# Moving page loads between the queues of a decoder-step kernel, and a threshold chain inside a projection

## The chip, the cores and the metric

The kernel is one program on one core of a Trainium2 chip. The metric is the device time of one execution in microseconds (us), lower is better. TensorE (PE) multiplies, VectorE (DVE) and ScalarE (ACT) do elementwise work, GpSimd (POOL) does elementwise work too, and SyncE (SP) computes nothing: it issues transfers. Here SP, ScalarE and GpSimd all issue transfers from their own instruction streams, and an engine that issues a transfer does nothing else during that time.

## The reference, cut to what matters

The program is one inference step of a two-layer decoder for a prompt (1024 tokens) and for 8 sample sequences of 8 new tokens each. Only the sample part of the sparse attention (DSA) in layer 0 is touched:

```python
def dsa_sample(layer, q, k_new, v_new, iq, ik_new, iw, cache_k, cache_v, cache_idx, page_table):
    ik_past = cache_idx[layer, page_table].reshape(Bd, PAST_LEN, IDX_DIM)   # 8 x 16 pages of 128 keys
    ik_all = jnp.concatenate([ik_past, ik_new], axis=1)
    sc = indexer_scores(iq, iw, ik_all)            # sum over 8 heads of weight * relu(iq . ik)
    _, idx = lax.top_k(sc, 256)                    # the 256 best of 2056 keys for each query
    ...
    return dsa_attend(q, ks, vs, idx <= t)         # softmax attention over the chosen keys
```

The pages of keys, values and index keys lie in a pool in HBM, and `page_table` says which page belongs where. The kernel doesn't gather the 256 keys: it finds the threshold (with ties counted), makes a bias of 0 or -1e30 for each of the 2056 keys, and attends to all of them under this bias.

## The kernel before, in words

Each stage of the program is a block: every engine runs its own instruction list, and all five meet at a barrier at the block's end. Three blocks matter.

**First block of `even_in` (line 266).** The input projection x @ w_in is cut into 12 chunks of weight columns, `PROJ`; this block multiplies the first `CW` = 9 of them. Each chunk has `KD` = 8 blocks of 128 input rows, and each block is 5 units on TensorE (two token tiles to a unit, the last unit has one): 360 units in all. For every block ScalarE makes the high part of the weights (`split_hi`, L207) and VectorE the low part (`split_lo`, L212) into a ring of `RING` = 4 slots. The helper `projection(n)` on VectorE or ScalarE emits the splits and evictions that are due when TensorE is at unit n: a split for block g once block g - 3 is reached. So the order in which VectorE's work stands between the splits is written out by hand. Between the units TensorE also computes the sample's index scores: for 16 steps m it transposes pages of index keys (L404), two sequences to four steps (`ix_in[b]` says that the 16 pages of sequence b have landed), multiplies them with the queries (L413) and adds the heads (L420). Then VectorE searches the 256 largest scores of each half row in 32 rounds (L513, L514), with `projection` calls between the rounds; it ends at unit `SEARCH` + 128 = 321. GpSimd then exchanges the two halves' lists (L360, semaphore `oth_in`), and VectorE makes the bias in a chain of 17 operations (L523 to L541), each waiting for the one before. GpSimd stores the bias to DRAM (L362) and waits for it (`b_out`). In this block the SP queue loads the weights of the chunks (`load_w`, L182), stores chunks 0 and 1 from a buffer of four slots (`store_stage`, L187), and loads the index pages of sequences 3 and 5; GpSimd loads those of 0, 1, 2, 4, 6 and 7.

**Second block of `even_in` (line 581)** multiplies the last three chunks beside the prompt's linear attention (GLA).

**`dsa_sample` (block at line 1592)** attends for the sample. Sequences go in four pairs p. For each pair TensorE transposes the key pages (`keys_T`, L1645) into two banks that ScalarE and VectorE empty (`copy_keys`, L1587), computes the scores with the bias (L1664, L1667), then already transposes the keys of the next pair, then transposes the probabilities (L1681) and multiplies the values (L1696, L1697). For each sequence there are 16 key pages and 16 value pages of 64 KB. `load_pages` (L54) loads them: in a loop over groups of four it reads four page numbers out of the page table into registers (`value_load`, L57) and issues four transfers (L61). The key pages of sequences 0, 2, 4, 6 and 7 and the value pages of 6 and 7 are on SP; those keys of 1, 3 and 5 are on ScalarE (`load_odd`), between its copies; the values of 0 to 5 are on GpSimd. Key and value buffers have four slots, so from sequence 4 on a load waits until the slot's old pages were transposed (`kt_done`) or multiplied (`y_done`). SP also loads the spread matrix, the bias and the new values between its keys.

Of the kernel before, what the change touches and what calls it, by code (L numbers as in the profile page):

```python
# [17 lines left out]
KD = D // P  # L18
# [18 lines left out]
TOPK = 256  # L37
# [4 lines left out]
PAGES = 16  # L42
# [10 lines left out]

def load_pages(eng, pages, n_pool, b, j0, j1, cache, dst_of, landed):  # L54
    group = 4
    with eng.Fori(j0 // group, j1 // group) as g:
        at = [eng.value_load(pages[0:1, bass.ds(g * group + (b * PAGES + r), 1)], min_val=0, max_val=n_pool - 1) for r in range(group)]  # L57
        for r in range(group):
            src = cache[bass.ds(at[r], 1)]
            src = src.rearrange("o p k d -> (o p) (k d)") if len(src.shape) == 4 else src.rearrange("o p d -> (o p) d")  # L60
            eng.dma_start(dst_of(bass.ds(g * group + r, 1)), src).then_inc(landed, 16)  # L61
# [40 lines left out]
def even_in(nc, st, A, C, O, x_tile, H, Hs):  # L102
# [35 lines left out]
    with ExitStack() as ctx:  # L138
# [127 lines left out]
        with ExitStack() as early, nc.Block() as block:  # L266
# [27 lines left out]
            def index_slot(p):  # L294
                return (idxb[:, 0], idxb[:, 1], staged_keys, idxb[:, 0])[p]

            def load_index(eng, b, j0, j1):
                load_pages(eng, pages, n_pool, b, j0, j1, A["cache_idx"][0],
                           lambda j: index_slot(b // 2)[:, j, b % 2, :].rearrange("p o d -> p (o d)"), ix_in[b])

# [5 lines left out]
            def _(sp):  # L306
# [15 lines left out]
                for c in range(1, CW + 1):  # L322
                    load_w(sp, c)
                    if c == 1:
                        sp.wait_ge(t_done, 2 * TILES)
                        load_index(sp, 3, 0, PAGES)
# [4 lines left out]
                    if c == 3:  # L331
                        sp.wait_ge(evac, NB * 3)
                        sp.dma_start(scr_w, Hs[0:NS, C_IW:C_IW + 8]).then_inc(w_out, 16)
                        sp.wait_ge(w_out, 16)
                        for f in range(2):
                            for h in range(8):
                                sp.dma_start(iwd[NS * f + 8 * h:NS * f + 8 * h + 8, :],
                                             bass.AP(scr_w.tensor, NS * f + h, [[8, 8], [2 * NS, NB2]]),
                                             allow_slow_non_contiguous=True).then_inc(iw_in, 16)
                        wait_staged(sp)  # L340
                        load_index(sp, 5, 0, PAGES // 2)
                    elif c == 4:
                        load_index(sp, 5, PAGES // 2, PAGES)
                sp.wait_ge(cin, 96)

            @block.gpsimd
            def _(pool):
                pool.wait_ge(pin, 16)
                load_index(pool, 0, 0, PAGES)
                load_index(pool, 1, 0, PAGES)  # L350
                pool.wait_ge(t_done, 2 * TILES)
                load_index(pool, 2, 0, PAGES)
                wait_staged(pool)
                load_index(pool, 4, 0, PAGES)
                pool.wait_ge(it_done, NQ)
                load_index(pool, 6, 0, PAGES)
                load_index(pool, 7, 0, PAGES)
                pool.wait_ge(lst_done, 1)
                for f in range(2):
                    pool.dma_start(oth[NS * f:NS * f + NS, :], lst[NS * (1 - f):NS * (1 - f) + NS, :]).then_inc(oth_in, 16)  # L360
                pool.wait_ge(b_done, 1)
                pool.dma_start(st.bias_dram, bias[:, :]).then_inc(b_out, 16)  # L362
                pool.wait_ge(b_out, 16)

# [112 lines left out]
            def _(dve):  # L477
# [38 lines left out]
                dve.sem_inc(lst_done, 1)  # L516
                projection(NB * KD * CW)
                for k in range(RING):
                    split_lo(dve, nc.vector.tensor_tensor, CW, k)
                dve.wait_ge(oth_in, 32)  # L520
# [13 lines left out]
                link(nc.vector.reduce_sum(more[:, :], hit[:, :], AX_X))  # L534
                link(nc.vector.tensor_tensor(num[:, :], num[:, :], more[:, :], ALU.subtract))
                equal, count = wk[:, :], relb[:, :, :].rearrange("p a n -> p (a n)")
                link(nc.vector.tensor_scalar(equal, sc[:, :], thr[:, 0:1], None, ALU.is_equal))
                link(nc.vector.tensor_tensor_scan(count, ones[:, 0:1].to_broadcast([P, LH]), equal, 0.0, ALU.mult, ALU.add))
                link(nc.vector.scalar_tensor_tensor(out=equal, in0=count, scalar=num[:, 0:1], in1=equal, op0=ALU.is_le, op1=ALU.mult))
                link(nc.vector.scalar_tensor_tensor(out=equal, in0=sc[:, :], scalar=thr[:, 0:1], in1=equal, op0=ALU.is_gt, op1=ALU.add))  # L540
                nc.vector.tensor_scalar(bias[:, :], equal, -1.0, -NEG, ALU.add, ALU.mult).then_inc(b_done, 1)  # L541

        gsb = lambda n, s, d=F32: ctx.enter_context(nc.sbuf_tensor(f"gla_{n}", s, d))
# [996 lines left out]
def dsa_sample(nc, st, A, C, O, Hs, XT):  # L1540
# [7 lines left out]
    with ExitStack() as ctx:  # L1548
# [39 lines left out]

        def load(eng, b, j0, j1, cache, dst, slot, landed):
            load_pages(eng, pages, n_pool, b, j0, j1, cache, lambda j: dst[:, slot, j, :].rearrange("p o c -> p (o c)"), landed)  # L1590

        with nc.Block() as block:
            @block.sync
            def _(sp):
                sp.dma_start(pages[:, :], A["page_table"].rearrange("(o a) b -> o (a b)", o=1)).then_inc(pin, 16)
                sp.wait_ge(pin, 16)
                load(sp, 0, 0, PAGES, A["cache_k"][0], Kp, 0, k_in[0])
                for f in range(2):
                    sp.dma_start(spf[NS * f:NS * f + NS, :, :], C["spread"]).then_inc(cin, 16)
                sp.dma_start(bias[:, :], st.bias_dram).then_inc(bias_in, 16)  # L1600
                for b in range(NB):
                    sp.dma_start(Vn[:, b, :], Hs[8 * b:8 * b + 8, C_DV:C_DV + P]).then_inc(vn_in, 16)
                for b in (2, 4, 6, 7):
                    if b >= 4:
                        sp.wait_ge(kt_done, 4 * (b - 3))
                    load(sp, b, 0, PAGES, A["cache_k"][0], Kp, b % 4, k_in[b % 4])
                sp.wait_ge(y_done, NP_ - 2)
                for b in range(NB - 2, NB):
                    load(sp, b, 0, PAGES, A["cache_v"][0], Vp, b % 4, v_last_in[b % 2])

            @block.gpsimd
            def _(pool):
                pool.wait_ge(pin, 16)
                for b in range(4):
                    load(pool, b, 0, PAGES, A["cache_v"][0], Vp, b % 4, v_in[b % 4])
                for p in range(NP_):
                    pool.wait_ge(y_done, p + 1)
                    for b2 in range(2):
                        pool.dma_start(bass.AP(scr_y.tensor, (2 * p + b2) * DEC_SEQ * 512, [[HD, 8], [512, DEC_SEQ], [1, HD]]),
                                       yq[64 * b2:64 * b2 + 64, p, :]).then_inc(y_out, 16)  # L1620
                        if p + 3 < NP_:
                            load(pool, 2 * p + 4 + b2, 0, PAGES, A["cache_v"][0], Vp, (2 * p + b2) % 4, v_in[(2 * p + b2) % 4])
                pool.wait_ge(y_out, 32 * NP_)
# [82 lines left out]
            def _(act):  # L1706
# [7 lines left out]
                act.wait_ge(h_c, 3)  # L1714
                act.wait_ge(pin, 16)

                def load_odd(b, j0, j1):
                    if b >= 4 and j0 == 0:
                        act.wait_ge(kt_done, 4 * (b - 3))
                    load(act, b, j0, j1, A["cache_k"][0], Kp, b % 4, k_in[b % 4])  # L1720

                load_odd(1, 0, PAGES)

# [5 lines left out]
                new_keys(0)  # L1729
                load_odd(3, 0, PAGES)  # L1730
                for g in range(8):
                    copy_keys(act, nc.scalar.copy, g)
                for p in range(NP_):
# [5 lines left out]
                    if p + 1 < NP_:  # L1739
                        act.wait_ge(s_done, p + 1)  # L1740
                        new_keys(p + 1)
                        for g in range(8 * p + 8, 8 * p + 16, 2):
                            copy_keys(act, nc.scalar.copy, g)
                        if p == 0:
                            load_odd(5, 0, PAGES)
                act.wait_ge(yt_done, 1)
# [1361 lines left out]
```

## Time and profile before

| | us |
|---|---|
| median of 3 runs | 3800.31 (3798.08 to 3800.9) |
| the profiled execution | 3798.53, span 3796.9 |
| first block of `even_in`, from its first projection product | 34.7 to 340.7 of the span |
| second block of `even_in` | 340.7 to 627.7 |
| `dsa_sample` | 627.7 to 814.6 |
| prompt attention, `dsa_out` | 814.6 to 1513 |
| the rest: feed-forward twice, odd layer | 1513 to 3796.9 |
| TensorE busy over the span | 3327.2 (88%) |
| VectorE, ScalarE, GpSimd busy | 42%, 29%, 10% |

In the timeline a row gives the start, the length, the engine, the line and the operation, with `out<-in` in the program's names; what stands in brackets is the time that the engine sat idle before it and who ended that. A row with x16 merges 16 instructions, and its length runs from the first one's start to the last one's end. SPq, ACTq and POOLq are the engines' instruction queues.

### The profile page before, as it was taken

The page shows a single profiled execution, that of the slowest core. Times are in us where ns is not written, and L with a number is a line of the kernel's source. Part 1 is how long each engine was busy: PE and PEld are TensorE (multiplying, and loading weights), DVE is VectorE, ACT ScalarE, POOL GpSimd, SP SyncE. Part 2 cuts the span into 40 slices and gives each one's busy share as a digit, 9 for nine tenths or more (in the row PEclk, how much of TensorE's full clock was granted, in tenths as well). Part 3 has the DMA queues.
Part 4 walks back from the last instruction along what each step waited for, and adds up shares of the span by engine and source line. Part 5 has one row for each costly group of instructions (what it writes and reads, how often), then busy time and mean ns, then how long its engine had stood idle before and what let it go on. Part 6 is the DMA issues. An engine that isn't in the chain of part 4 may idle for free. (4 is left out here: it accounts for less than half of the span.)

```text
span 3796.9 us, 53619 instructions
## 1 busy us (share of the span) xinstructions
PE 3327.2 (88%) x20601; PEld 2834.1 (75%) x20627; DVE 1601.5 (42%) x2851; ACT 1095.4 (29%) x2144; POOL 394.2 (10%) x507
## 2 busy tenths in 40 slices
PE   8996884668878887999999998896997999999997
PEld 7796674434444443999999998893665999999997
DVE  2184762216777782211112565331554211112566
ACT  2223442122333332211112443212443211112443
POOL 2200112321111100000000001350000000000002
PEclk9998885867788887999999999896999999999999
DMA  4111004440000000111112110213001111112111
GB/s 139 45 34 30 23 12 129 113 146 12 20 20 20 12 12 28 50 44 44 44 44 93 40 56 34 52 54 111 20 34 39 45 44 44 44 44 91 40 58 48
DMA packets 232358, 190.76 MB, mean 50 GB/s; under 512 B 49538, under 2 KB 210580, under 8 KB 232148
## 3 DMA queue, kind: packets, MB, share of 16 engines
q1 hardware_dynamic: 216436, 166.17, 14.5%
q0 software_dynamic: 8832, 19.02, 1.6%
q10 hardware_dynamic: 6912, 3.15, 0.3%
q8 instruction: 118, 1.93, 0.2%
q14 instruction: 60, 0.49, 0.0%
HBM read 158.64 MB, written 31.38 MB: 50 GB/s over the span
## 5 line engine op out<-in xcount | busy, mean ns | idle before, releaser
L1885 PE MATMUL ffn1u_ps<-h_hi,ffn1u_whi 128*128 128x384 f32 (+1 forms) x1056 | 348.5, 330 | 8.7 <-DVE h_lo L1947 8.7
L1885 PE MATMUL ffn0u_ps<-h_hi,ffn0u_whi 128*128 128x384 f32 (+1 forms) x1056 | 344.9, 327 | 8.6 <-DVE h_lo L1947 8.6
L1885 PE MATMUL ffn1u_ps<-h_lo,ffn1u_whi 128*128 128x384 f32 (+1 forms) x1056 | 348.3, 330 | 0.0
L1885 PE MATMUL ffn1u_ps<-h_hi,ffn1u_wlo 128*128 128x384 f32 (+1 forms) x1056 | 348.3, 330 | 0.0
L1885 PE MATMUL ffn0u_ps<-h_hi,ffn0u_wlo 128*128 128x384 f32 (+1 forms) x1056 | 345.1, 327 | 0.0
L1885 PE MATMUL ffn0u_ps<-h_lo,ffn0u_whi 128*128 128x384 f32 (+1 forms) x1056 | 344.9, 327 | 0.0
L196 PE MATMUL ine_ps<-ine_w_hi,ine_x_hi 128*128 128x256 f32 (+2 forms) x864 | 264.9, 307 | 4.6 <-DVE ine_w_lo L212 4.6
L196 PE MATMUL ine_ps<-ine_w_hi,ine_x_lo 128*128 128x256 f32 (+2 forms) x864 | 250.3, 290 | 0.0
L196 PE MATMUL ine_ps<-ine_w_lo,ine_x_hi 128*128 128x256 f32 (+2 forms) x864 | 249.6, 289 | 0.0
L1885 PEld LDWEIGHTS ffn1u_ps<-h_hi,ffn1u_whi 128*128 128x128 f32 x1056 | 199.2, 189 | 9.1 <-DVE ffn1u_wlo L1929 9.1
L1885 PEld LDWEIGHTS ffn0u_ps<-h_hi,ffn0u_whi 128*128 128x128 f32 x1056 | 198.7, 188 | 8.9 <-DVE ffn0u_wlo L1929 8.9
L1885 PEld LDWEIGHTS ffn1u_ps<-h_lo,ffn1u_whi 128*128 128x128 f32 x1056 | 199.1, 189 | 0.0
L1885 PEld LDWEIGHTS ffn1u_ps<-h_hi,ffn1u_wlo 128*128 128x128 f32 x1056 | 199.1, 189 | 0.0
L1885 PEld LDWEIGHTS ffn0u_ps<-h_hi,ffn0u_wlo 128*128 128x128 f32 x1056 | 198.6, 188 | 0.0
L1885 PEld LDWEIGHTS ffn0u_ps<-h_lo,ffn0u_whi 128*128 128x128 f32 x1056 | 198.6, 188 | 0.0
L2033 PE MATMUL ffn0d_ps<-ffn0d_w_hi,ffn0d_a_hi 128*128 128x256 f32 (+1 forms) x594 | 171.6, 289 | 12.9 <-DVE ffn0d_X L2135 6.5
L2033 PE MATMUL ffn1d_ps<-ffn1d_w_hi,ffn1d_a_hi 128*128 128x256 f32 (+1 forms) x594 | 171.2, 288 | 12.9 <-DVE ffn1d_X L2135 6.5
L196 PEld LDWEIGHTS ine_ps<-ine_w_hi,ine_x_hi 128*128 128x128 f32 (+1 forms) x864 | 167.2, 194 | 17.3 <-issue 8.6
L196 PEld LDWEIGHTS ine_ps<-ine_w_hi,ine_x_lo 128*128 128x128 f32 (+1 forms) x864 | 167.4, 194 | 4.1 <-issue 4.1
L2033 PE MATMUL ffn0d_ps<-ffn0d_w_hi,ffn0d_a_lo 128*128 128x256 f32 (+1 forms) x594 | 170.1, 286 | 0.0
L2033 PE MATMUL ffn0d_ps<-ffn0d_w_lo,ffn0d_a_hi 128*128 128x256 f32 (+1 forms) x594 | 170.0, 286 | 0.0
L2033 PE MATMUL ffn1d_ps<-ffn1d_w_hi,ffn1d_a_lo 128*128 128x256 f32 (+1 forms) x594 | 169.7, 286 | 0.0
(441 smaller groups left out, 7418.2 us busy)
## 6 DMA issues: line engine op xcount, KB each, us to landing
ffn0u_raw<-in_ffn_w_gu_dram SPq DMA_DIRECT2D x44, 512.0 KB, 3.8
ffn1u_raw<-in_ffn_w_gu_dram SPq DMA_DIRECT2D x44, 512.0 KB, 3.8
ffn0d_w<-in_ffn_w_down_dram SPq DMA_DIRECT2D x88, 128.0 KB, 2.1
ffn1d_w<-in_ffn_w_down_dram SPq DMA_DIRECT2D x88, 128.0 KB, 2.2
smp_Vp<-in_cache_v_dram POOLq DMA_DIRECT2D x96, 64.0 KB, 2.2
ine_w<-in_w_in_even_dram SPq DMA_DIRECT2D x5, 1024.0 KB
scratch_h<-ine_stage SPq DMA_DIRECT2D x20, 256.0 KB, 2.5
smp_Kp<-in_cache_k_dram SPq DMA_DIRECT2D x80, 64.0 KB, 2.0
```

The source lines that it names most:

```text
L196: last = nc.tensor.matmul(o, xp[:, k, i * P:i * P + r], wp[:, g % RING, 0:n], start=(k == 0 and j == 0 and i % 2 == 0), stop=(k == KD - 1 ...
L1885: last = nc.tensor.matmul(ps[:, t, k2, 0:n], wp[:, k2, k, :], hp[:, k, t0:t0 + n], start=(k == 0 and j == 0), stop=(k == KD - 1 and j == 2))
L2033: last = nc.tensor.matmul(acc(i), ap[:, n % 2, i * P:i * P + rows(i)], wp[:, k, :], start=(k == 0 and j == 0 and i % 2 == 0), stop=(k == K ...
```

## The change

The threshold chain of 17 VectorE operations is cut in two and put among the splits of the ninth chunk (`CW` - 1), instead of after all of them. The bias is stored to DRAM by SP, not by GpSimd. The index pages of sequences 1 and 7 move from GpSimd to SP, and GpSimd loads its own in groups of one page. In `dsa_sample` SP issues all key pages; ScalarE issues none.

```diff
-def load_pages(eng, pages, n_pool, b, j0, j1, cache, dst_of, landed):
-    group = 4
+def load_pages(eng, pages, n_pool, b, j0, j1, cache, dst_of, landed, group=4):
...
             def _(sp):
...
                     if c == 1:
+                        load_index(sp, 1, 0, PAGES)
                         sp.wait_ge(t_done, 2 * TILES)
                         load_index(sp, 3, 0, PAGES)
...
                     elif c == 4:
                         load_index(sp, 5, PAGES // 2, PAGES)
+                        sp.wait_ge(it_done, NQ)
+                        load_index(sp, 7, 0, PAGES)
+                sp.wait_ge(b_done, 1)
+                sp.dma_start(st.bias_dram, bias).then_inc(b_out, 16)
+                sp.wait_ge(b_out, 16)
                 sp.wait_ge(cin, 96)
             def _(pool):
                 pool.wait_ge(pin, 16)
-                load_index(pool, 0, 0, PAGES)
-                load_index(pool, 1, 0, PAGES)
+                load_index(pool, 0, 0, PAGES, 1)
                 pool.wait_ge(t_done, 2 * TILES)
-                load_index(pool, 2, 0, PAGES)
+                load_index(pool, 2, 0, PAGES, 1)
                 wait_staged(pool)
-                load_index(pool, 4, 0, PAGES)
+                load_index(pool, 4, 0, PAGES, 1)
                 pool.wait_ge(it_done, NQ)
-                load_index(pool, 6, 0, PAGES)
-                load_index(pool, 7, 0, PAGES)
+                load_index(pool, 6, 0, PAGES, 1)
...
-                pool.wait_ge(b_done, 1)
-                pool.dma_start(st.bias_dram, bias[:, :]).then_inc(b_out, 16)
-                pool.wait_ge(b_out, 16)
...
                 dve.sem_inc(lst_done, 1)
-                projection(NB * KD * CW)
-                for k in range(RING):
-                    split_lo(dve, nc.vector.tensor_tensor, CW, k)
+                projection(SEARCH + 4 * (TOPK // 8) + NB)
                 dve.wait_ge(oth_in, 32)
...
                 link(nc.vector.tensor_tensor(num[:, :], num[:, :], more[:, :], ALU.subtract))
+                projection(SEARCH + 4 * (TOPK // 8) + 3 * NB)
...
                 nc.vector.tensor_scalar(bias[:, :], equal, -1.0, -NEG, ALU.add, ALU.mult).then_inc(b_done, 1)
+                projection(NB * KD * CW)
+                for k in range(RING):
+                    split_lo(dve, nc.vector.tensor_tensor, CW, k)
...
                 load(sp, 0, A["cache_k"][0], Kp, 0, k_in[0])
+                load(sp, 1, A["cache_k"][0], Kp, 1, k_in[1])
...
-                for b in (2, 4, 6, 7):
+                for b in range(2, NB):
...
-                act.wait_ge(pin, 16)
-                def load_odd(b, j0, j1):
-                    if b >= 4 and j0 == 0:
-                        act.wait_ge(kt_done, 4 * (b - 3))
-                    load(act, b, j0, j1, A["cache_k"][0], Kp, b % 4, k_in[b % 4])
-                load_odd(1, 0, PAGES)
                 new_keys(0)
-                load_odd(3, 0, PAGES)
...
-                        if p == 0:
-                            load_odd(5, 0, PAGES)
```

## Rows read from the trace of the kernel before

**Rows 1.** Stage table: length, busy time (x instructions) by engine, granted clock, DMA share, GB/s.
```profile
34.70:340.70 306.00, 274.35 (x2097) 249.51 (x2097) 132.76 (x213) 61.98 (x165) 42.38 (x79) 0.96 0.19 50
627.70:814.60 186.90, 98.56 (x581) 69.39 (x581) 34.75 (x62) 21.79 (x40) 56.65 (x105) 0.76 0.34 95
```
**Rows 2.** Timeline of TensorE where the first block ends.
```profile
340.78 0.37 PE L632 MATMUL ine_ps<-ident,H 128*16 128x128 f32 x1 [24.75 <-PEq L266]
```
**Rows 3.** Timeline of VectorE there: last splits, and three of the chain's 17 operations.
```profile
316.95 1.43 DVE L212 TENSOR_TENSOR ine_w_lo<-ine_w,ine_w_hi 128x256 fp32r<-128x256 f32 x4 [12.87 <-ACT ine_w_hi L207]
318.30 0.28 DVE L523 COPY idx_rel<-idx_rel 128x256 f32<-128x256 f32 x1
...
322.56 0.76 DVE L537 TENSOR_SCALAR idx_wk<-idx_sc,idx_thr 128x1032 f32<-128x1032 f32 x1
...
328.35 0.70 DVE L541 TENSOR_SCALAR idx_rel<-idx_wk 128x1032 bf16<-128x1032 f32 x1
```
**Rows 4.** Timeline of GpSimd: the lists' exchange and the bias's store.
```profile
298.98 1.07 POOL L360 DMA_DIRECT2D idx_rel<-idx_lst  x2 [118.20 <-DVEq L516]
329.35 0.59 POOL L362 DMA_DIRECT2D scratch_bias<-idx_rel  x1 [29.30 <-DVE idx_rel L541]
```
**Rows 5.** Line 266, the block's end (duration ns min/median/max, first and last start us).
```profile
L266 POOLq DRAIN  x1: 8149/8149/8149, 332.3 to 332.3; - x1
```
**Rows 6.** Timeline of TensorE: first products of blocks 69 and 71.
```profile
306.23 0.28 PE L196 MATMUL ine_ps<-ine_w_hi,ine_x_hi 128*128 128x256 f32 x1
...
312.66 0.28 PE L196 MATMUL ine_ps<-ine_w_hi,ine_x_hi 128*128 128x256 f32 x1
```
**Rows 7.** Timeline of TensorE: the thirteenth transpose of index pages.
```profile
182.31 0.63 PE L404 MATMUL ine_ps<-ident,idx_keys 128*128 128x128 f32 x4 [2.32 <-DMA idx_keys<-in_cache_idx_dram]
```
**Rows 8.** Timeline of GpSimd: four pages of index keys of sequence 6.
```profile
144.43 2.47 POOL L61 DMA_DIRECT2D idx_keys<-in_cache_idx_dram  x4 [2.90 <-issue]
```
**Rows 9.** Timeline of SP's queue in the first block.
```profile
37.05 19.39 SPq L61 DMA_DIRECT2D idx_keys<-in_cache_idx_dram  x16
60.15 2.52 SPq L187 DMA_DIRECT2D scratch_h<-ine_stage  x4
62.71 2.76 SPq L182 DMA_DIRECT2D idx_w<-in_w_in_even_dram  x3
```
**Rows 10.** Tile idx_w, loads from 62 to 66 us.
```profile
DMA to landing us min/median/max: 3.5/4.6/4.9
```
**Rows 11.** Timeline of ScalarE: it evicts the second chunk.
```profile
85.24 2.74 ACT L233 COPY ine_stage<-ine_ps 128x512 f32<-128x512 f32 x4 [0.39 <-PE ine_ps L196]
```
**Rows 12.** Timeline of SP's queue in `dsa_sample`.
```profile
632.07 17.37 SPq L61 DMA_DIRECT2D smp_Kp<-in_cache_k_dram  x16
...
651.49 5.54 SPq L1602 DMA_DIRECT2D smp_Vn<-Hs  x8
660.30 18.35 SPq L61 DMA_DIRECT2D smp_Kp<-in_cache_k_dram  x16
...
746.23 18.37 SPq L61 DMA_DIRECT2D smp_Vp<-in_cache_v_dram  x16
...
767.66 19.59 SPq L61 DMA_DIRECT2D smp_Vp<-in_cache_v_dram  x16
```
**Rows 13.** Line 57 in `dsa_sample`: a page number is read.
```profile
L57 SPq TENSOR_LOAD <-smp_pages x112: 262/264/598, 629.2 to 784.1; - x112
```
**Rows 14.** DMA issues in `dsa_sample`: line, count, KB each, median us to landing.
```profile
smp_Vp<-in_cache_v_dram SPq DMA_DIRECT2D x32, 64.0 KB, 1.9
```
**Rows 15.** Timeline of TensorE in `dsa_sample`.
```profile
672.88 0.48 PE L1645 MATMUL smp_ps<-ident,smp_Kp 128*128 128x128 f32 x1 [19.58 <-ACT smp_KT L1587]
...
766.23 6.28 PE L1696 MATMUL smp_ps<-smp_Vp,smp_PT 128*64 128x128 f32 x32 [4.94 <-DMA smp_Vp<-in_cache_v_dram]
...
793.99 3.71 PE L1696 MATMUL smp_ps<-smp_Vp,smp_PT 128*64 128x128 f32 x32
797.63 0.43 PE L1697 MATMUL smp_ps<-smp_Vn,smp_PT 8*64 8x128 f32 x2
```

More of the change, by code:

```diff
@@ L295, in index_slot, with load_index @@
                 return (idxb[:, 0], idxb[:, 1], staged_keys, idxb[:, 0])[p]
-            def load_index(eng, b, j0, j1):
+            def load_index(eng, b, j0, j1, group=4):
                 load_pages(eng, pages, n_pool, b, j0, j1, A["cache_idx"][0],
-                           lambda j: index_slot(b // 2)[:, j, b % 2, :].rearrange("p o d -> p (o d)"), ix_in[b])
+                           lambda j: index_slot(b // 2)[:, j, b % 2, :].rearrange("p o d -> p (o d)"), ix_in[b], group)
             def wait_staged(eng):
@@ L1587, in copy_keys, with load @@
             op(KT[:, g // 4 % 2, 512 * (g % 4):512 * (g % 4 + 1)], ps[:, 5 + g % 2, :]).then_inc(key_copy(g)[0], 1)
-        def load(eng, b, j0, j1, cache, dst, slot, landed):
-            load_pages(eng, pages, n_pool, b, j0, j1, cache, lambda j: dst[:, slot, j, :].rearrange("p o c -> p (o c)"), landed)
+        def load(eng, b, cache, dst, slot, landed):
+            load_pages(eng, pages, n_pool, b, 0, PAGES, cache, lambda j: dst[:, slot, j, :].rearrange("p o c -> p (o c)"), landed)
         with nc.Block() as block:
@@ L1596, in _ @@
                 sp.wait_ge(pin, 16)
-                load(sp, 0, 0, PAGES, A["cache_k"][0], Kp, 0, k_in[0])
+                load(sp, 0, A["cache_k"][0], Kp, 0, k_in[0])
+                load(sp, 1, A["cache_k"][0], Kp, 1, k_in[1])
                 for f in range(2):
@@ L1602, in _ @@
                     sp.dma_start(Vn[:, b, :], Hs[8 * b:8 * b + 8, C_DV:C_DV + P]).then_inc(vn_in, 16)
-                for b in (2, 4, 6, 7):
+                for b in range(2, NB):
                     if b >= 4:
                         sp.wait_ge(kt_done, 4 * (b - 3))
-                    load(sp, b, 0, PAGES, A["cache_k"][0], Kp, b % 4, k_in[b % 4])
+                    load(sp, b, A["cache_k"][0], Kp, b % 4, k_in[b % 4])
                 sp.wait_ge(y_done, NP_ - 2)
                 for b in range(NB - 2, NB):
-                    load(sp, b, 0, PAGES, A["cache_v"][0], Vp, b % 4, v_last_in[b % 2])
+                    load(sp, b, A["cache_v"][0], Vp, b % 4, v_last_in[b % 2])
             @block.gpsimd
@@ L1614, in _ @@
                 for b in range(4):
-                    load(pool, b, 0, PAGES, A["cache_v"][0], Vp, b % 4, v_in[b % 4])
+                    load(pool, b, A["cache_v"][0], Vp, b % 4, v_in[b % 4])
                 for p in range(NP_):
@@ L1621, in _ @@
                         if p + 3 < NP_:
-                            load(pool, 2 * p + 4 + b2, 0, PAGES, A["cache_v"][0], Vp, (2 * p + b2) % 4, v_in[(2 * p + b2) % 4])
+                            load(pool, 2 * p + 4 + b2, A["cache_v"][0], Vp, (2 * p + b2) % 4, v_in[(2 * p + b2) % 4])
                 pool.wait_ge(y_out, 32 * NP_)
```

## The prediction

> **What bounds the kernel now.** I read the stage table first, to see where TensorE isn't the limit. The line to notice is `dsa_sample`: 186.9 us with TensorE busy for 98.6, while VectorE, ScalarE and GpSimd are each busy for 57 us or less, and the transfers' share is 0.34 [rows 1]. No engine's work and no bandwidth fills this stage, so something that the busy columns don't count does. In the first block TensorE is busy 274 of 306 us [rows 1]; there only holes are to be won. Then I read the timeline at the first block's end: TensorE sat idle for 24.75 us until the second block began at 340.78 [rows 2]. Walk back from there. GpSimd's instruction queue shows a DRAIN of 8.15 us from 332.3 to 340.45 [rows 5]. Before that it stored the bias, issued at 329.35 and waited for until 332.3 [rows 4, 5]. The bias came from VectorE's chain, 318.30 to 329.05, and this stood behind the last weight splits, which ended at 318.38 [rows 3]. So the hole is a chain of splits, threshold chain, store, and drain. Last, I read SP's queue in `dsa_sample`: it goes from one batch of 16 pages to the next without a pause [rows 12].
>
> **The threshold chain.** It moves into the ninth chunk. It needs the exchanged lists, issued by 300.05 [rows 4]; with the 1.9 us that a 64 KB transfer takes to land [rows 14], about 302, and the rest of the window up to 316 has VectorE nearly empty. Its first part (12 operations) takes 318.30 to 322.56 = 4.3 us, its second 322.56 to 329.05 = 6.5 us [rows 3]. Started at 301.5 to 302, the first part ends at 306. Now the splits: with `projection(326)` block 68 is split ahead of it, 69 and 70 follow it, 71 follows the second part. TensorE reaches block 69 at 306.23 and block 71 at 312.66 [rows 6]. 69 is just in time, or late by 0.2. The second part runs from 306.5 to 313.0, and block 71's split (four took 1.43 [rows 3]) comes at 313.4: TensorE waits 0.8 us. All later work of the block moves by 0.8, so the last split ends at 319.2. SP has nothing else to do by then; its store of the bias begins at 313.1 and is confirmed by 316.1, taking the 3 us of GpSimd's [rows 4, 5]. GpSimd's last transfer is now the exchange at 300.05, and its drain of 8.15 us, if it is as long there, ends near 309, under the products. The barrier took 0.33 from the drain's end to TensorE's start [rows 2, 5]. TensorE starts at 319.5 and not at 340.8: **-21.3 us**. The idle time shrinks from 24.75 to some 3. Value products after 4.94 us of idle took 6.28, those without 3.71 [rows 15], so the first products of the second block may win 0 to 2.6; I take -1.0, since a short idle time shows it too.
>
> **Index pages.** TensorE waited 2.32 us at its thirteenth step for the pages of sequence 7, which GpSimd loaded last [rows 7]. Now SP issues them behind sequence 5's, some 20 us before they are needed, and GpSimd ends with sequence 6. It pays for a group of one: four pages took 5.37 us (2.47 + 2.90) [rows 8], and has 12 more loop turns for 16 pages. In the 2.90 us four page numbers are read, at no less than SP's 0.264 each [rows 13], and one turn is made, so a turn costs between 0 and 1.8; I take an estimate of 0.5, since the reads need register operations too, and a batch is 6 us longer. Sequence 6, begun at 136.2 and 21.5 long, would end by 164, 16 us before step 13; at 1.8 a turn it would end at 179 and the gain would be gone. I take **-2.3 us**. But SP is moved past its own stores and weights. After sequence 1's pages (in the place of 3's, to 56.44) it issues those of 3, 21.7 us more (below): to 78.2. Only then come the stores of chunk 0, before at 60.15, and the weights of chunk 2, before at 62.71 [rows 9]. Four stores whose data is ready take 2, the three weight issues 2.76: to 82.9, landed at 86.4 to 87.8 by 3.5 to 4.9 us each [rows 10]. ScalarE's program has the first splits of chunk 2 ahead of its evictions of chunk 1, which began at 85.24 [rows 11]. It would begin them three splits (0.3 each) after landing, at 87.5. TensorE needs the first bank when it is through chunk 1, at about 87.7, with the copy of 0.6 to 0.7 done: a wait of 0.4 in the middle, 0 to 3.5 at the bounds. I take **+0.5**. The stores of chunk 0 land by 84, ahead of those evictions, which need their slots.
>
> **Key pages.** ScalarE issued 48 pages in three batches and held up its copies; the row to see is TensorE's wait of 19.58 us for a copy, until 672.88 [rows 15]. That stall goes. What is late next is the same moment: sequence 1's keys now come second on SP, ending at 649.44 + 21.7 = 671.2 and landing at 673. So nothing is won for the first pair, and three batches are added to SP. What does a batch cost on this queue? From the last issue of sequence 2 (678.65) to the last of value sequence 7 (787.25) SP issued 5 batches without a wait: 108.6 / 5 = 21.72 us, 1.36 a page [rows 12]. This is instruction time: reading one page number takes 0.264 us for the load alone [rows 13], and register operations and the issue come on top. SP's list is then: sequence 0 to 649.44 as before, sequence 1 to 671.2, spread, bias and new values 7.6 (649.44 to 657.03) to 678.8, and 8 batches more (keys 2 to 7, values 6 and 7), 173.8, to 852.5. Before it was 787.25, so +65.2. Its waits (`kt_done`, `y_done` at 2) are long met then: keys of 6 would be issued from 765, when those of sequence 2, landed at 702, are transposed. Sequence 7's keys land at 811; transposes, the third pair's probabilities and values, the fourth's scores and softmax are some 37 us more as in the timeline of before, to 848 or so, and the last value pages land at 852.5 + 1.9 = 854.4 [rows 14]. So these are last. In the trace of before they weren't: landed at 789.2, and their product began at 793.99 [rows 12, 15]. After the wait that product takes 6.3 + 0.3 [rows 15] and ends at 861.0 instead of 798.06: **+62.9 us**. GpSimd's value pages, waiting on pair 0's and 1's products, fall back too but land 25 us before their use. The tail of the stage is unchanged.
>
> **A rule weighed.** The row shows 21.7 us for 16 pages of 64 KB [rows 12], each landing in 1.9 [rows 14]: issue, not movement. The Trainium skill, page "DMA: Bandwidth & Descriptors", section "Issuing engines are not separate DMA queues", says that issuing on several engines at once saves only the sequencer's time, "usually small relative to the DMA itself". By that rule the batches moved would cost nothing, which is the second rival below. The trace speaks against it in this case.
>
> **The sum.** On the profiled execution: 3798.5 - 21.3 - 1.0 - 2.3 + 0.5 + 62.9 = 3837.3. The median of the runs is 1.8 above that execution, so 3839.
>
> **The rivals.**
> 1. *The queue runs faster alone.* If ScalarE's issues slowed SP's, ten batches would take 17.37 + 3.27 = 20.6 each (the shortest length, and 657.03 to 660.30 before it [rows 12]); SP ends at 843: 3829. Against it: from 746.23 to 767.66 ScalarE issued nothing, and the pitch was 21.4 [rows 12].
> 2. *Not slower: the key pages are hidden.* The place is the last value pages on SP. If SP had slack of over 63 us there, or the copies freed on ScalarE gave it back, the stage would keep its length: 3839 - 62.9 = 3776. It decides once a batch costs under about 8 us (the gain of 24 over three). For it speaks only the stall of 19.58 [rows 15]; against it the unbroken queue.
> 3. *Weights of chunk 2 late.* Landing 4 us later adds 4 and some products at the lower clock, up to +7: 3846.
> 4. *The drain or the store ends the block after all.* If GpSimd's drain begins only when the others are done, 8 of the 21.3 come back: 3847; if none of the hole goes, 3860.
>
> **Chances.** My forecast 0.71 (3832 to 3846), rival 1 0.10, rival 3 0.07, rival 4 0.07, rival 2 0.05. The range: below, rival 1 with a margin for the clock, 3826; above, rivals 3 and most of 4, 3851. A difference under about 0.2% (8 us) can't be told from none here. Slower than that 0.94, within it 0.02, faster 0.04.
>
> **What would show it.** TensorE's idle time before L632 of 3 us; a wait of some 0.8 before the last block's products; no wait at the thirteenth L404; SP's page transfers in `dsa_sample` as ten batches at a pitch of 21.7 without pauses; TensorE waiting on `smp_Vp` from SP at the end, and on `smp_Kp` before each pair from the second on. I am wrong if SP shows pauses there, if a batch takes well under 20 us, or if the stage ends by anything else.

## The result, and the profile after

The changed kernel takes **3838.97 us** (median; 3836.47 to 3862.03), against 3799.19 of the kernel before (3790.54 to 3800.9, measured beside it): a ratio of 1.0122 with a 95% interval of 1.0086 to 1.0157: slower, by 1.2%. A second comparison gave 3837.37 against 3798.3, 1.0107 (1.0093 to 1.0122). The prediction was 3839. The profiled execution took 3838.52, with a span of 3836.9 against 3796.9, so 40.0 us are to be found.

The stage table of after, for the same two stages as [rows 1] (start and end, length, busy time by engine, granted clock, DMA share, GB/s):

```profile
34.70:316.00 281.30, 274.04 (x2097) 249.14 (x2097) 132.79 (x214) 61.41 (x165) 26.45 (x50) 0.99 0.21 55
602.90:852.90 250.00, 108.69 (x581) 76.69 (x581) 35.23 (x62) 22.07 (x40) 56.68 (x105) 0.66 0.25 71
```

TensorE did the same work in the first block (274 us), in 281 us instead of 306. In `dsa_sample` it did the same instructions in 250 us instead of 187; its busy time grew by 10, with a mean granted clock of 0.66 instead of 0.76 of full speed. The engine waits more, and works slower after waits (the same 32 products took 6.58 us behind a wait, below, and 3.71 elsewhere).

**The first block's end.** Timelines of VectorE, TensorE, SP's queue and GpSimd, and the line of GpSimd's DRAIN, the last instruction of its list in a block (duration ns, then first and last start):

```profile
298.06 0.29 DVE L521 COPY idx_rel<-idx_rel 128x256 f32<-128x256 f32 x1 [2.02 <-DMA idx_rel<-idx_lst]
...
302.34 0.76 DVE L211 TENSOR_TENSOR ine_w_lo<-idx_w,ine_w_hi 128x256 fp32r<-128x256 f32 x2
303.02 0.75 DVE L536 TENSOR_SCALAR idx_wk<-idx_sc,idx_thr 128x1032 f32<-128x1032 f32 x1
...
308.80 0.70 DVE L540 TENSOR_SCALAR idx_rel<-idx_wk 128x1032 bf16<-128x1032 f32 x1
309.42 0.42 DVE L211 TENSOR_TENSOR ine_w_lo<-idx_w,ine_w_hi 128x256 fp32r<-128x256 f32 x1
...
314.28 1.43 DVE L211 TENSOR_TENSOR ine_w_lo<-ine_w,ine_w_hi 128x256 fp32r<-128x256 f32 x4 [4.45 <-ACT ine_w_hi L206]
```
```profile
309.89 0.39 PE L195 MATMUL ine_ps<-ine_w_hi,ine_x_hi 128*128 128x256 f32 x1 [0.37 <-DVE ine_w_lo L211]
316.05 0.27 PE L634 MATMUL ine_ps<-ident,H 128*16 128x128 f32 x1 [2.69 <-PEq L265]
```
```profile
309.52 0.34 SPq L347 DMA_DIRECT2D scratch_bias<-idx_rel  x1
```
```profile
295.61 1.06 POOL L363 DMA_DIRECT2D idx_rel<-idx_lst  x2 [136.11 <-DVEq L516]
```
```profile
L265 POOLq DRAIN  x1: 6080/6080/6080, 296.1 to 296.1; - x1
```

The chain now stands among the splits and is over at 309.5, while TensorE still multiplies. TensorE's idle time before the second block is 2.69 us where [rows 2] had 24.75. The DRAIN still takes 6.08 us, but from 296.1 on, beside the products. The second block begins at 316.05 and not at 340.78: 24.7 us won.

**`dsa_sample`.** SP's queue, then the waits of TensorE (us in total, times, longest), then its last rows:

```profile
607.27 40.13 SPq L60 DMA_DIRECT2D smp_Kp<-in_cache_k_dram  x32
...
658.25 125.77 SPq L60 DMA_DIRECT2D smp_Kp<-in_cache_k_dram  x96
787.48 40.55 SPq L60 DMA_DIRECT2D smp_Vp<-in_cache_v_dram  x32
```
```profile
PE smp_ps L1648 <- DMA smp_Kp<-in_cache_k_dram: 101.7, 7, 22.7
...
PE smp_ps L1699 <- DMA smp_Vp<-in_cache_v_dram: 5.3, 1, 5.3
```
```profile
829.51 6.58 PE L1699 MATMUL smp_ps<-smp_Vp,smp_PT 128*64 128x128 f32 x32 [5.32 <-DMA smp_Vp<-in_cache_v_dram]
836.02 0.43 PE L1700 MATMUL smp_ps<-smp_Vn,smp_PT 8*64 8x128 f32 x2
```

SP goes through ten batches without a pause (in the gaps of some 3 us it reads the first page numbers of the next group); from the end of the new values (654.99) to its last issue (828.03) the last eight took 173.0 us, 21.6 a batch. TensorE waited seven times for key pages, 101.7 us in all, and at the end for the last value pages, as forecast. From the block's first transpose to its last product it was 233.05 us (602.97 to 836.02) against 169.85 (627.78 to 797.63, [rows 15]): 63.2 lost. -24.7 + 63.2 is 38.5 of the 40.0. The other 1.5 lie behind these stages, where it can't be placed: from the first transposes of the prompt's attention to the span's end it was 2974.9 us before and 2976.6 after, and between 2972.3 and 2979.7 in the experiments, which change nothing there.

### The profile page after: what moved, and what is told of

Read it like the earlier page. It is cut to its first block and busy times, and to the rows that moved or that the text cites. A ratio compares the mean times of both kernels' runs of the same rounds, so it can differ in the third digit from the quotient of the medians.

```text
span 3836.9 us, 53726 instructions
## 1 busy us (share of the span) xinstructions
PE 3341.4 (87%) x20627; PEld 2841.1 (74%) x20627; DVE 1602.3 (42%) x2851; ACT 1095.6 (29%) x2143; POOL 376.5 (10%) x474
```

## The experiments

Each is compared with the kernel before, run beside it on the same chip.

**The two halves apart.** First the changed kernel with `dsa_sample` as before:

```diff
-                load(sp, 1, A["cache_k"][0], Kp, 1, k_in[1])
...
-                for b in range(2, NB):
+                for b in (2, 4, 6, 7):
...
+                load_odd(1, 0, PAGES)
...
+                load_odd(3, 0, PAGES)
...
+                            load_odd(5, 0, PAGES)
```


> The changed kernel with dsa_sample as it was before (key pages of sequences 1, 3 and 5 on ScalarE): the part of the change in the first block alone. My theory (two independent parts, first block -24.7 us as the trace of after shows, dsa_sample +63.2): TensorE begins the second block at 316, dsa_sample is again 170.3 us long, and the time is 3799.2 - 24.7 = 3774.5, up to 1.7 more if the small rise in the later stages comes from the first part too. Rival (the gain of the first block is given back later, because the later stages start their transfers earlier and meet other traffic or a lower clock): above 3785.

Measured: **3770.98 us** (3770.08 to 3774.68) against 3797.2, ratio 0.9932 (0.9915 to 0.9948): -26.2, 3.5 under the expected 3774.5. Then the kernel before with `dsa_sample` of after, the same edit the other way round:

> The kernel before with only dsa_sample changed: all key pages on SP. My theory: ten batches in a row on SP, +63.2 us, 3862.4. Rival (key pages are hidden, and the loss came from something else, for instance the bias or the barrier arriving at another moment): near 3799. Where the two parts add, this difference and that of the run with the first part alone sum to +39.8, the change's own.

Measured: **3857.96 us** (3856.95 to 3861.63) against 3797.2, ratio 1.0165 (1.0148 to 1.0182): +60.8 (expected: +63.2). So the change holds a gain and a loss, each in its place, and neither is given back elsewhere. The two sum to +34.6, 4.5 less than the change's own +39.1 (second comparison; 39.8 in the first). The traces show where such an amount lies: the unchanged code of `dsa_sample` took 169.85 us in the profiled execution of before, but 165.63 in the run with the first part alone, and 165.47 and 165.72 in two runs further down. In the trace of before, TensorE's wait for sequence 5's values was 4.94 us and the products behind it took 6.28 ([rows 15]), against 3.69 and 5.33 with the first part alone; the value products from 788.10 on took 5.61 against 3.71, with a granted clock of 0.70 there and 1.00 in the other. That makes 4.1 of the 4.2 us. Why the clock was lower there isn't settled; the same code took 167.17 us in the run with the bias stored by GpSimd. So against the first part alone the key pages cost 67.4 us (233.05 - 165.63), and against before 61.2 (keys-only run, 231.05) to 63.2.

**How far SP's list decides.** The last two batches of SP's list to GpSimd:

```diff
-                sp.wait_ge(y_done, NP_ - 2)
-                for b in range(NB - 2, NB):
-                    load(sp, b, A["cache_v"][0], Vp, b % 4, v_last_in[b % 2])
...
+                    if p == 1:
+                        for b in range(NB - 2, NB):
+                            load(pool, b, A["cache_v"][0], Vp, b % 4, v_last_in[b % 2])
```


> The changed kernel with the last two batches of SP's list in dsa_sample (value pages of sequences 6 and 7) issued by GpSimd after pair 1's values. SP then issues 8 batches and ends with the keys of sequence 7, at 784 as before. My theory: SP's queue sets the time twice, at each pair's keys and at the last values; with the values gone only the last wait (5.32 us) and the slower products behind it (6.58 for 3.71) are won, and the stage ends 8.2 us earlier: 3831. GpSimd's two batches end near 800 and land ahead of their use at 818. Rival A (only the length of SP's list counts, 21.7 us a batch): -43, 3796. Rival B (GpSimd's batches are later than SP's were): at or above 3839.

Measured: **3826.8 us** (3822.61 to 3845.08), ratio 1.0078 (1.0061 to 1.0095); about 11 less than the changed kernel. The stage was 223.60 us long in the trace, 9.45 less than after (expected: 8.2). Two batches of 21.6 us off the queue gave 9, because the keys of sequence 7, from the same queue, were next by 5 us. The value pages were last, but only just; what costs the 63 us is the whole row of key pages.

**Issue or transfer.** The same number of transfers of the same size, but from fixed places, so that SP reads no page number (this leaves the page table out for all key pages and the last value pages):

```diff
+            if eng is nc.sync:
+                for j in range(PAGES):
+                    src = cache[b * PAGES + j:b * PAGES + j + 1]
+                    src = src.rearrange("o p k d -> (o p) (k d)")
+                    eng.dma_start(dst[:, slot, j, :], src).then_inc(landed, 16)
+                return
```


> The changed kernel with SP's pages in dsa_sample fetched from fixed places in the caches, in the same number and size, so that no page number is read, no register is worked on and there is no loop: it leaves the page table out for the key pages and the last value pages. My theory (SP's instructions set the 1.36 us of a page): a batch of 16 takes about 8 us (0.5 each, as fixed transfers on SP elsewhere), keys are there early, and GpSimd's value pages at 23 us a batch are next: the stage ends 60 to 92 us earlier, 3747 to 3779. Rival (the transfers or their rings set the pace, not the instructions): batches of over 17 us, and 3839 or little under it.

Measured: **3769.38 us** (3768.38 to 3771.5), ratio 0.9929 (0.9912 to 0.9945). SP's queue in this run, and one of TensorE's waits:

```profile
603.78 15.52 SPq L1596 DMA_DIRECT2D smp_Kp<-in_cache_k_dram  x32
...
627.10 46.68 SPq L1596 DMA_DIRECT2D smp_Kp<-in_cache_k_dram  x96
702.07 16.09 SPq L1596 DMA_DIRECT2D smp_Vp<-in_cache_v_dram  x32
```
```profile
739.65 5.24 PE L1705 MATMUL smp_ps<-smp_Vp,smp_PT 128*64 128x128 f32 x32 [14.28 <-DMA smp_Vp<-in_cache_v_dram]
```

96 pages are issued in 46.68 us, 0.49 each instead of 1.35, and SP's ten batches now cost less than before's seven. Both the stage (165.54 us) and the time are some 68 us shorter than the changed kernel's. So neither bandwidth nor the transfers' own queues set the pace, but the 0.86 us that reading the page number, its register work and the loop add to each issue. What is left waits on GpSimd, which still reads page numbers (14.28 us before its value pages), as the expectation has it.

**The DRAIN's price.** The first part alone, with the bias stored by GpSimd again:

```diff
-                sp.wait_ge(b_done, 1)
-                sp.dma_start(st.bias_dram, bias).then_inc(b_out, 16)
-                sp.wait_ge(b_out, 16)
...
+                pool.wait_ge(b_done, 1)
+                pool.dma_start(st.bias_dram, bias[:, :]).then_inc(b_out, 16)
+                pool.wait_ge(b_out, 16)
```


> The first-block part alone (3770.98), with one piece of it undone: the bias is stored by GpSimd again, which waits for it, and not by SP. The threshold chain stays in the ninth chunk. My theory: GpSimd's DRAIN starts when its last transfer is confirmed and has a length of its own of 6 to 8.6 us. The bias is ready at 309.5, the store is confirmed at 312.5, the DRAIN ends at 318.6 to 320.7, and the second block starts there and not at 316: +2.9 to +5.0, 3774 to 3776. Rival (the DRAIN only waits for transfers that are open, so it is short once they are confirmed): no difference, 3771.

Measured: **3772.69 us** (3771.0 to 3775.8), 1.7 over the first part alone, at equal ratios (0.9932; 0.9916 to 0.9949), so the time alone doesn't decide it. The trace does:

```profile
L265 POOLq DRAIN  x1: 5536/5536/5536, 313.4 to 313.4; - x1
```
```profile
319.24 0.27 PE L634 MATMUL ine_ps<-ident,H 128*16 128x128 f32 x1 [4.93 <-PEq L265]
```

The DRAIN begins once the store is confirmed, takes 5.54 us, and the second block begins right at its end, 2.6 us later than with SP's store (316.65; expected: 2.9 to 5.0). So it has a length of its own, and with the chain already moved, the store's move is worth 2 to 3 us, not 8.

**The late weights.** The profiled execution of the run with value pages on GpSimd took 3845.08, 18 us over that kernel's median. TensorE's row where chunk 2 begins, and windows of this trace (start and end, length, busy times by engine, granted clock, DMA share, GB/s):

```profile
90.43 0.31 PE L195 MATMUL ine_ps<-ine_w_hi,ine_x_hi 128*128 128x152 f32 x1 [2.51 <-ACT ine_stage L232]
```
```profile
80.00:91.00 11.00, 8.49 (x72) 8.26 (x71) 0.77 (x3) 1.95 (x6) 0.00 (x0) 1.00 0.63 160
91.00:102.00 11.00, 11.00 (x63) 11.00 (x63) 0.95 (x3) 1.85 (x6) 2.14 (x4) 0.57 0.62 200
102.00:135.00 33.00, 33.00 (x164) 33.00 (x164) 3.00 (x8) 4.24 (x15) 6.42 (x12) 0.50 0.05 14
```

The weights of chunk 2, which SP issues behind sequence 3's pages, were late; TensorE waited 2.51 us and then worked at the lower of its two clock levels (0.50 of full speed, 1.2 GHz), from about 92.5 to 137 us. In the same 33 us the run with the first part alone, at full clock, issued 242 matmuls and not 164. To force it, sequence 3's pages in groups of one on SP (`load_index(sp, 3, 0, PAGES, 1)`), on the first part alone:

> The first-block part alone (3770.98), with sequence 3's index pages on SP read one by one (12 more loop turns of 0.43 us), so that the weights of chunk 2 behind them land 5 us later, at some 93 where they landed at 88.02. It tests what the 2.04 us wait at chunk 2 turns into. My theory, from the profiled execution of the run with value pages on GpSimd (a wait of 2.51 us there, then the granted clock at 0.50 from 91 to 136 us): every execution waits 7 us and then multiplies at the lower clock for some 45 us, +5 and +20: 3796. Rival (the clock had another cause and only the wait counts): +5, 3776.

Measured: **3769.7 us** (3768.7 to 3792.09), ratio 0.9922 (0.9906 to 0.9939): as a forced delay it failed. A loop turn cost less than I had put (the batch took 3.0 us more, not 5.2) and it began 1.8 earlier, so the weights landed at 89.52, only 1.5 later. But one of five executions, the profiled one, took 3792.09, and its trace has a wait and the same windows:

```profile
90.88 0.31 PE L195 MATMUL ine_ps<-ine_w_hi,ine_x_hi 128*128 128x152 f32 x1 [1.33 <-ACT ine_stage L232]
```
```profile
102.00:135.00 33.00, 33.00 (x164) 33.00 (x164) 2.47 (x7) 4.23 (x15) 6.75 (x13) 0.50 0.05 14
```

My "every execution" is wrong: a wait of 1.33 us was followed by the lower clock, waits of 2.04, 2.01 and 1.02 us at the same place (first part alone, index pages alone, bias on GpSimd) weren't. One thing sets the two apart in these traces: TensorE went on later, at 90.43 and 90.88 against 89.37, 90.14 and 89.74; five cases are too few to call that the reason. The cure to try is to issue the weights first:

```diff
                         load_index(sp, 1, 0, PAGES)
+                    if c == 2:
                         sp.wait_ge(t_done, 2 * TILES)
                         load_index(sp, 3, 0, PAGES)
```


> The first-block part alone (3770.98), with SP issuing the stores of chunk 0 and the weights of chunk 2 ahead of sequence 3's index pages, not behind them. The weights land near 65. My theory: the wait of 2.04 us before chunk 2's first bank goes, nothing else is late (sequence 3's pages land near 86, and TensorE needs them after 140): 3769, and no execution 20 us over the others. Rival (the pages or chunk 1's stores behind them become late): 3771 or more.

Measured: **3771.16 us** (3770.76 to 3773.86), ratio 0.9929 (0.9913 to 0.9946). SP's queue has the weights at 64.38, 16 us ahead of after's 80.80, and the wait is gone, but the 2 us of it don't show in the median: the expected 3769 missed, and the number is the rival's (3771 or more), though TensorE waits for nothing new in this block's trace. The same edit on the changed kernel, with the changed kernel beside it:

> The changed kernel itself again, as the mate of the next run. My theory: most executions within 4 us of 3838, and some (one of four so far) 20 to 24 us longer with a mean granted clock lower by 0.006, those in which the late weights of chunk 2 end in 44 us at the lower clock. Rival (the long execution of before was a chance event that has nothing to do with the weights): none here, or as many in the next run.

> The changed kernel with SP issuing the stores of chunk 0 and the weights of chunk 2 ahead of sequence 3's index pages. My theory: no wait at chunk 2, so no execution with the 44 us at the lower clock there; median 0 to 2 us under the changed kernel's. Rival (see the run of the changed kernel): long executions here too.

Measured: **3837.37 us** (3834.78 to 3838.54; ratio 1.0107, 1.0093 to 1.0122) and **3836.45 us** (3835.97 to 3838.29; 1.0105, 1.009 to 1.0119). No long execution in either, so this pair decided nothing. Counted over all runs of this study, the seven kernels with the weights behind the pages had 5 long executions of 42 (18 to 24 us over their kernel's median; 3862.03 of the changed kernel is one), the four with the weights first none of 16. Two of the five have a trace, and both show the lower clock behind that wait. With before's first block, in which the weights land in time, none of 39 was long. Five long ones among 97 would all fall among those 42 by chance in about one case of 75. But the 42 differ from the 39 in all that moving the index pages did; the fair contrast for the weights is with the 16, and five long ones among these 58 would all miss the 16 in about one case of 5. So the count doesn't settle it: that the late weights make the long executions is what the two traces point to, and it isn't shown.

**Index pages alone**, on the kernel before:

```diff
                     if c == 1:
+                        load_index(sp, 1, 0, PAGES)
...
+                        sp.wait_ge(it_done, NQ)
+                        load_index(sp, 7, 0, PAGES)
...
-                load_index(pool, 1, 0, PAGES)
...
-                load_index(pool, 7, 0, PAGES)
```


> The kernel before with the index pages alone moved (sequences 1 and 7 to SP, groups of one on GpSimd). My theory: the wait of 2.32 us at the thirteenth step goes, and the wait at chunk 2 (0 to 2 us) comes: 1.8 to 3.3 us faster than before, a ratio of 0.9991 to 0.9995, and most of the 26 us of the first-block part belongs to the threshold chain. Rival (the two edits need each other, since the bias and the lists share GpSimd's queue): over 5 us faster, or slower than before.

Measured: **3788.85 us** (3784.6 to 3813.16) against 3798.3, ratio 0.9987 (0.9974 to 1.0001): 9 us by the medians, with an interval that takes in none at all. The expectation (1.8 to 3.3) missed, and the medians lie where the rival had them (over 5 us), though the trace shows other reasons for it. The trace places 4.87 us in the first block: its VectorE chain begins 2.05 earlier, as expected, and GpSimd's DRAIN took 5.54 us where [rows 5] had 8.15, which I hadn't expected. Another 4.4 are the shorter `dsa_sample` (165.47), whose code is that of before; with 12 and 17 executions behind the two medians this is more than one trace's chance, but what would tie it to the edit isn't shown. The second block begins thus:

```profile
335.91 0.37 PE L632 MATMUL ine_ps<-ident,H 128*16 128x128 f32 x1 [21.93 <-PEq L265]
```

Of the 24.7 us of the first block, then, some 4.9 are the index pages' and some 20 the chain's and the store's.

**Another DRAIN, and the queues dealt out anew.** On the run with the weights first, the last pair's y goes by SP, which also reads all of y back at the end:

```diff
-                for p in range(NP_):
+                for p in range(NP_ - 1):
                     pool.wait_ge(y_done, p + 1)
...
+                sp.wait_ge(y_done, NP_)
+                for b2 in range(2):
+                    sp.dma_start(bass.AP(scr_y.tensor, (2 * NP_ - 2 + b2) * DEC_SEQ * 512, [[HD, 8], [512, DEC_SEQ], [1, HD]]),
+                                 yq[64 * b2:64 * b2 + 64, NP_ - 1, :]).then_inc(y_last_out, 16)
```


> As the run with the weights first, and in dsa_sample the last pair's two stores of y and the load that reads them back go to SP, so that GpSimd's last transfer is pair 2's store. My theory: GpSimd's DRAIN of 8.6 us, which ends the block of dsa_sample in the trace of before and of after, begins some 35 us earlier and is hidden; the next block starts 7 to 8.6 us sooner: 3760.5 to 3762 (against 3769). Rival (other engines' ends, or the transfers that the next block starts with, are as late): 3767 to 3769.

Measured: **3763.3 us** (3761.71 to 3764.26), ratio 0.9906 (0.989 to 0.9923), 7.9 less than without the edit. GpSimd's DRAIN at this block's end was 9.12 us long and began at 747.8, ahead of the last products; SP's, at 775.6, took 7 ns. TensorE's wait before the next block's first transposes, without the edit and with it:

```profile
794.01 1.97 PE L1207 MATMUL dsa_ps<-ident,dsa_KI 128*128 128x128 f32 x8 [16.21 <-DMA dsa_KI<-scratch_h]
```
```profile
785.40 1.97 PE L1207 MATMUL dsa_ps<-ident,dsa_KI 128*128 128x128 f32 x8 [8.81 <-DMA dsa_KI<-scratch_h]
```

Last, each queue keeps the page numbers that it has read:

```diff
+            def read(eng, b):
+                return [eng.value_load(pages[0:1, b * PAGES + j:b * PAGES + j + 1], min_val=0, max_val=n_pool - 1) for j in range(PAGES)]
...
+                at0 = keys(sp, 0)
...
+                at2 = keys(sp, 2)
+                values(sp, 0, at0)
...
+                at3 = keys(pool, 3)
+                values(pool, 1, read(pool, 1))
+                at5 = keys(pool, 5)
+                values(pool, 3, at3)
```


> The run with y on SP (3763.3), with the paged transfers of dsa_sample dealt out anew: a queue that has read a sequence's 16 page numbers keeps them in registers for the keys and, later, for the values (SP has sequences 0, 2, 4, 6, GpSimd 3, 5, 7 and sequence 1's values, ScalarE only sequence 1's keys, before it has copies to make), without a loop. Working: on SP 16 numbers read take 10.4 us (0.65 each) and 16 issues 9.1 (0.57), so keys and values of a sequence take 28.6 and not 43.4; both keys of the first pair land near 630 (ScalarE's copies aren't held until 648), pair 1's near 649, pair 2's at 683, pair 3's at 712, and from there it is 46 us to the last product, as in the run of the first-block part. My theory (instructions of the issuing queues are the limit): dsa_sample ends 9 to 14 us earlier: 3749 to 3754. Rival (GpSimd, with two sequences' keys on its queue, is late with them, or reading 16 numbers in a row is no cheaper): 3763 or more.

Measured: **3742.06 us** (3741.84 to 3742.98), ratio 0.9856 (0.9842 to 0.987): 56 us under the kernel before, 95 under the changed one. SP's queue and two of TensorE's waits for keys:

```profile
623.89 0.59 SPq L1626 DMA_DIRECT2D smp_bias<-scratch_bias  x1
633.40 8.68 SPq L1602 DMA_DIRECT2D smp_Kp<-in_cache_k_dram  x16
642.18 7.75 SPq L1602 DMA_DIRECT2D smp_Vp<-in_cache_v_dram  x16
```
```profile
644.20 4.37 PE L1684 MATMUL smp_ps<-ident,smp_Kp 128*128 128x128 f32 x20 [5.02 <-DMA smp_Kp<-in_cache_k_dram]
...
702.66 1.09 PE L1684 MATMUL smp_ps<-ident,smp_Kp 128*128 128x128 f32 x8 [0.66 <-DMA smp_Kp<-in_cache_k_dram]
```

Between the bias (done 624.48) and the next keys (633.40) SP reads 16 page numbers: 8.9 us, 0.56 each, where I had put 0.65. The 16 value pages behind them need no reading and take 7.75, 0.48 each: an issue whose address is already in a register costs no more than one with a fixed address, so what the run with fixed places saved was the reading and the loop. Behind the first keys of the stage, the longest wait for keys has shrunk from 18.9 us to 5.0, and the stage is 145.03 us long, 20.7 less than in the run before it (165.77). I had expected 9 to 14; the direction held, the size didn't.

## Why the prediction was right, point by point

- **The chain.** Forecast: the second block begins 21.3 (chain) + 2.3 (index pages) - 0.5 (weights) = 23.1 us earlier; it was 24.7. The lists' exchange came 3.4 us earlier than in [rows 4], where the forecast has 1.8 (2.3 less 0.5): the weights' wait of 0.5 wasn't there, and a wait of TensorE for VectorE at L420 was 1.41 us and not 2.17; the two parts of the chain took what they had taken before (4.3 and 6.5 us); TensorE's wait before the last block was 0.37 us and not 0.8; SP confirmed the bias by 311.9, long before the last split.
- **The DRAIN.** Assumed as long as before (8.15 us) and hidden. It was hidden, and 6.08 us long. Rival 4 priced it at 8 us; the run with GpSimd's store says 2 to 3, since with the chain moved the block's other work ends only 2.6 us before that DRAIN does.
- **The clock**, -1.0: not there. The second block took 287.0 us before and 286.9 after.
- **Index pages.** No wait at the thirteenth step; SP's stores of chunk 0 began at 78.7 (forecast 78.2), the weights were issued by 83.8 (82.9) and landed at 87.2 (86.4 to 87.8); GpSimd's sequence 6 ended at 159.5 (by 164).
- **Chunk 2's weights**, +0.5: the step with a wrong upper bound. I had 0 to 3.5 us for the wait, and up to +7 with the clock (rival 3). The wait was 0 in the profiled execution of after and 1.0 to 2.5 in other kernels, but about one execution of eight with this order was some 20 us longer, behind that wait in the two that have a trace. The median doesn't feel it. One execution in four of the first comparison was long, 3862.03, which lies above the stated range of 3826 to 3851; it has no trace.
- **First pair.** Nothing won, as forecast: sequence 1's keys were transposed from 649.04, 46.1 us into the stage, after a wait of 18.92 us for the transfer; before, TensorE waited 19.58 for ScalarE until 45.1 us into it.
- **Three batches on SP.** Forecast +65.2 on the queue at 21.72 a batch, last value pages landed 226.7 us after the block's start, then a product of 6.3 + 0.3: +62.9. Measured: 21.6 a batch, landed 226.5 after it, 6.58 + 0.43: +63.2. Rival 1 (a queue that is faster alone) falls with the 21.6; rival 2 (key pages hidden) falls with the keys-only run, +60.8. The Trainium skill's rule from the prediction (page "DMA: Bandwidth & Descriptors", section "Issuing engines are not separate DMA queues") speaks of an initiation that is usually small relative to the transfer; this case differs, since 0.86 of 1.35 us a page went when the page numbers weren't read, and 68 us of the time with them.
- **How near the sum came.** On the profiled execution it was 3837.3, measured 3838.5. That the two agree to 1.2 us is in part luck: the first block won 1.6 us more than forecast, the 1.0 of the clock wasn't there, `dsa_sample` lost 0.3 more, and 1.5 came from stages that the change doesn't touch. One stage alone varies by more than that: with all key pages on SP and the same lists, `dsa_sample` took 231.05 to 233.35 us in four traces. What the forecast had right without luck are the two mechanisms and their sizes to some 2 us each.

## What to carry to other kernels

Count the instructions of an issuing queue as you count those of an engine: a transfer whose address is read from a table costs the reading, the register work and the issue, and a queue with no pause in the trace is a bound, though no busy column shows it. Before transfers go from three queues to two, cheapen the issue, for instance by reading an address once for all who use it. And let the last transfer of a block go through an engine whose end-of-block DRAIN is short (here SP: 7 ns, where GpSimd's took 5.5 us or more), and put what TensorE needs next ahead of bulk loads on a queue: in two traces a wait of 1 to 3 us was followed by 44 us at half clock.

## What the runs showed of the hardware that I hadn't expected

- The lower clock behind a short wait isn't decided by the wait's length alone: it came after 1.33 and 2.51 us, and not after 1.02, 2.01 and 2.04 at the same place. Both times it lasted some 44 us, with TensorE busy throughout, and the execution was 18 and 22 us over its kernel's median.
- GpSimd's DRAIN at the end of the first block and of `dsa_sample` had the same length to some 0.01 us in every run with the same program there (at the second block's end it varied, 7.64 to 7.83). It doesn't simply grow with the transfers that GpSimd issued in the block: 6.08 us with 66, 5.54 with 67, 8.15 with 99, 9.12 with 102, 8.64 with 105, 6.54 with 118, 7.33 with 137. It began when the engine's last wait was over, at 313.4 with the bias stored by GpSimd and at 296.1 without. What sets its length is open.
